# The low part of a projection weight block in eight operations of one K tile instead of four of two

## The chip, the cores and the metric

The kernel runs on one core of one Trainium2 chip. Measured is device time in microseconds of one execution of the program on that core. A chip has TensorE (PE, the matrix engine), VectorE (DVE), ScalarE (ACT), GpSimd (POOL) and SyncE (SP, which here only issues DMAs); each runs its own list of instructions in order, and they meet through semaphores.

## The reference

It is one inference step of a two-layer decoder trunk, for a prompt of 1024 positions and for 8 samples of 4 positions, which share all weights. Per layer: RMSNorm, one input projection from 1024 to 3592 columns, four token mixers beside one another (S5, HGRN2, mLSTM, retention), their gated outputs side by side, one output projection, and the residual:

```python
for l in range(DEPTH):                      # DEPTH = 2
    h = rmsnorm(x, norm_w[l])
    proj = jnp.einsum('bld,de->ble', h, w_in[l]).astype(f32)
    ...
    mixed = jnp.concatenate([s5_out * jax.nn.silu(s5_g), hg_out * jax.nn.silu(hg_g),
                             ml_out * jax.nn.silu(ml_g), rt_out * jax.nn.silu(rt_g)], axis=-1)
    x = x + jnp.einsum('ble,ed->bld', mixed.astype(x.dtype), w_out[l])
```

All of it is float32. The change touches the input projection alone.

## The kernel before

**Passes and blocks.** The prompt is cut into two halves of 512 positions, so there are four passes n = 0 to 3 (layer n // 2, half n % 2); the odd passes take the 32 sample positions along. A pass goes through 14 blocks of the input projection, each 256 columns wide (ml_ifg 264), in the order of the table BLOCKS; 4 x 14 = 56 blocks in all. `make_plan` writes down one order of steps for the whole kernel, and every engine walks through the same list and does its own share of each step.

**The split product.** TensorE multiplies in the type fp32r, and a projection is made of three products so as to keep float32's precision: the weights are split into a high part `whi` and a low part `wlo`, the rows into `hhi` and `hlo`, and for each K tile (128 of the 1024 input features; KT = 8 of them) the kernel adds hhi times whi, hhi times wlo and hlo times whi (lines 2270 to 2280). A block whose columns are channels ("ch") has the weights as the stationary operand and is done in pieces of up to 512 positions (line 2275); a "tok" block has the rows as the stationary operand and is done in pieces of 128 positions (line 2280). In the odd passes a "tok" block begins with the piece of the 32 sample positions, which multiplies the raw float32 weights `wraw` (line 2267). In the profile the trace prints the operands of the two lines 2275 and 2280 as out<-stationary,moving or the reverse; `whi`, `wlo`, `hhi` and `hlo` tell them apart.

**Who makes the parts.** ACT loads a block of weights by DMA into one of two slots of `wraw` (line 1149) and copies it as one operation into `whi` (line 1132, 128 x 2048, about 1.9 us); POOL subtracts, `wlo = wraw - whi`, in `split_low` (line 1088). Both go one block ahead of TensorE: `split_after` puts them at the first piece of the block before. `whi` and `wlo` have two slots each, so POOL first waits for the last piece of two blocks back, then for `whi`:

```python
                for g in range(4):
                    ks = slice(2 * g, 2 * g + 2)
                    nc.gpsimd.tensor_tensor(wlo[:, hslot[b], ks, 0:width], wraw[:, wslot[b], ks, 0:width],
                                            whi[:, hslot[b], ks, 0:width].bitcast(F32), ALU.subtract).then_inc(*wlo_done.inc(b + (g,)))
```

**Who waits for them.** TensorE waits for `wlo_done` in the first piece of a block, ahead of every second K tile (line 2263), also where this first piece is the sample piece, which doesn't read `wlo`. ACT waits for the last `wlo_done` of a block before it loads the next weights into that slot of `wraw` (line 1144, in `load_until`).

**What else POOL does.** In the order of the plan it computes `rstd` of a tile of rows for RMSNorm (lines 1097 and 1099; DVE's L1521 scales the rows with it, TensorE's L2245 transposes them, DVE's L1587 makes `hlo`), and `rs`, the scale of the head norm of a chunk of 128 positions (lines 1110 and 1113; DVE's L2195 multiplies `y` with it, after which TensorE's L2564 transposes `y`). Both are a short operation and a power. L1989, L2002 and L2010 are DVE's operations in the HGRN mixer; L1560 is one of the ml branch.

## Time and profile before

| | |
|---|---|
| median of 3 runs | 1610.68 us (1610.04 to 1617.34) |
| profiled execution, first to last instruction | 1609.6 us |
| its own time beside that span | not given apart; the span stands for it |
| mean granted TensorE clock | 0.919 |
| PE, PEld, DVE, ACT, POOL busy | 1387.8, 1214.1, 883.0, 524.2, 394.0 us |
| low parts on POOL (line 1088) | 224 operations, 297.1 us |
| high parts on ACT (line 1132) | 56 operations, 107.2 us |
| three products, line 2280 | 3 x 896 matmuls, 274.6 + 264.8 + 264.7 us |
| three products, line 2275 | 3 x 672 matmuls, 230.7 + 219.7 + 219.6 us |

How to read it: the times of an engine are what its instructions took; instructions of different engines overlap, and matmuls overlap one another on TensorE. In a row that ends in brackets, as [1.00 <-POOL wlo L1088], the engine stood idle for so many us before the instruction, and what follows the arrow ended this. The duration of a DVE or POOL operation includes the time in which it has begun and stands still. A row xN merges N instructions in a row.

### The profile page before, as it was taken

What the parts mean: (1) busy time and instruction counts of PE and PEld (TensorE: products, weight loads), DVE (VectorE), ACT (ScalarE), POOL (GpSimd) and SP (SyncE); (2) the same over time, 40 slices, a digit from 0 to 9 for tenths busy, and PEclk for the clock granted to TensorE, in tenths of its full rate; (3) what the DMA queues carried; (4) which work ended last, traced back from release to release, by engine and by line L of the source; (5) the groups of instructions that cost most, each with busy time, mean ns of one, the idle gap of its engine ahead of it and who ended that gap; (6) DMA issues with size and microseconds to landing.
All of it is one profiled execution on the core that took longest, in us unless ns stands there. A gap on an engine that the chain in (4) does not pass through costs nothing. (4 is left out here: it accounts for less than half of the span.)

```text
span 1609.6 us, 31327 instructions
## 1 busy us (share of the span) xinstructions
PE 1387.8 (86%) x12391; PEld 1214.1 (75%) x12391; DVE 883.0 (55%) x2652; ACT 524.2 (33%) x1093; POOL 394.0 (24%) x404
## 2 busy tenths in 40 slices
PE   3666899989897898898999989998989899789777
PEld 2566699788776787886777869877878798778546
DVE  5985736463795426455646442647365444644544
ACT  4335433333323422321443233233532433321011
POOL 4232233421001333140210144252200333231001
PEclk9888999979898999897999989998999999889879
DMA  6132123422233432372313323242313314359101
GB/s 183 59 98 68 53 81 105 138 75 90 65 107 107 112 74 76 94 127 44 106 65 95 117 77 107 82 152 67 115 50 113 106 56 120 137 82 201 54 9 57
DMA packets 167177, 149.83 MB, mean 93 GB/s; under 512 B 63440, under 2 KB 155352, under 8 KB 165240
## 3 DMA queue, kind: packets, MB, share of 16 engines
q1 hardware_dynamic: 96312, 76.38, 17.4%
q10 hardware_dynamic: 70720, 71.44, 15.4%
q8 instruction: 100, 1.64, 0.4%
q14 instruction: 45, 0.37, 0.1%
HBM read 124.42 MB, written 23.37 MB: 92 GB/s over the span
## 5 line engine op out<-in xcount | busy, mean ns | idle before, releaser
L1088 POOL TENSOR_TENSOR wlo<-wraw,whi 128x512 fp32r<-128x512 f32 (+1 forms) x224 | 297.1, 1357 | 434.0 <-ACT whi L1132 434.0
L2280 PE MATMUL psum<-whi,hhi 128*128 128x256 f32 (+1 forms) x896 | 274.6, 306 | 40.9 <-DVE r L1545 20.3
L2280 PE MATMUL psum<-wlo,hhi 128*128 128x256 f32 (+1 forms) x896 | 264.8, 296 | 0.0
L2280 PE MATMUL psum<-whi,hlo 128*128 128x256 f32 (+1 forms) x896 | 264.7, 295 | 0.0
L2275 PE MATMUL psum<-hhi,whi 128*128 128x288 f32 (+2 forms) x672 | 230.7, 343 | 2.9 <-DVE hlo L1587 1.6
L2280 PEld LDWEIGHTS psum<-whi,hhi 128*128 128x128 f32 x896 | 183.4, 205 | 49.2 <-issue 46.2
L2275 PE MATMUL psum<-hlo,whi 128*128 128x288 f32 (+2 forms) x672 | 219.7, 327 | 0.0
L2275 PE MATMUL psum<-hhi,wlo 128*128 128x288 f32 (+2 forms) x672 | 219.6, 327 | 0.0
L2280 PEld LDWEIGHTS psum<-wlo,hhi 128*128 128x128 f32 x896 | 183.3, 205 | 0.7 <-issue 0.5
L2605 PE MATMUL psum<-wraw,mixT 128*128 128x256 f32 x768 | 180.4, 395 | 4.0 <-DVE xo L2205 4.0
L2280 PEld LDWEIGHTS psum<-whi,hlo 128*128 128x128 f32 x896 | 182.6, 204 | 0.0
L1110 POOL TENSOR_SCALAR rs<-mv 128x4 f32<-128x4 f32 (+1 forms) x54 | 10.4, 192 | 665.6 <-DVE mv L2171 665.1
L2605 PEld LDWEIGHTS psum<-wraw,mixT 128*128 128x128 f32 x768 | 150.5, 199 | 27.1 <-DVE xo L2205 5.1
L1132 ACT ACTIVATE whi<-wraw 128x2048 fp32r<-128x2048 f32 (+1 forms) x56 | 107.2, 1915 | 115.1 <-PE psum L2275 44.0
L2275 PEld LDWEIGHTS psum<-hhi,whi 128*128 128x128 f32 x672 | 128.5, 191 | 18.3 <-issue 6.7
L2275 PEld LDWEIGHTS psum<-hhi,wlo 128*128 128x128 f32 x672 | 128.5, 191 | 11.8 <-issue 3.0
L2275 PEld LDWEIGHTS psum<-hlo,whi 128*128 128x128 f32 x672 | 128.1, 191 | 10.6 <-issue 0.2
L2168 DVE BATCH_NORM_STATS2 stats<-psum 128x6 f32<-128x64 f32 (+1 forms) x144 | 22.3, 217 | 105.9 <-PE psum L2526 105.9
L2526 PE MATMUL psum<-r,ST 128*128 128x64 f32 (+1 forms) x384 | 69.5, 285 | 3.8 <-issue 3.5
L1545 DVE SCALAR_TENSOR_TENSOR r<-th,psum 128x256 f32<-128x256 f32 (+3 forms) x72 | 24.9, 351 | 72.9 <-ACT th L1219 71.7
L2526 PEld LDWEIGHTS psum<-r,ST 128*128 128x128 f32 x384 | 58.0, 202 | 5.6 <-issue 5.3
L1989 DVE TENSOR_TENSOR r<-r 128x256 f32<-128x256 f32 (+1 forms) x134 | 51.6, 456 | 15.2 <-PE psum L2437 15.1
(351 smaller groups left out, 2277.5 us busy)
## 6 DMA issues: line engine op xcount, KB each, us to landing
wraw<-in_w_in ACTq DMA_DIRECT2D x50, 1024.0 KB, 5.4
wraw<-in_w_out ACTq DMA_DIRECT2D x14, 1024.0 KB, 5.4
x<-xo SPq DMA_DIRECT2D x48, 128.0 KB, 2.3
r<-x SPq DMA_DIRECT2D x10, 512.0 KB, 5.4
r<-in_c_rot SPq DMA_DIRECT2D x4, 1088.0 KB, 6.9
wraw<-in_w_in ACTq DMA_DIRECT2D x4, 1056.0 KB, 6.0
r<-WTm SPq DMA_DIRECT2D x4, 1024.0 KB, 12.7
r<-VTm SPq DMA_DIRECT2D x4, 1024.0 KB, 4.8
```

What stands on the lines that cost most here:

```text
L1088: nc.gpsimd.tensor_tensor(wlo[:, hslot[b], ks, 0:width], wraw[:, wslot[b], ks, 0:width], whi[:, hslot[b], ks, 0:width].bitcast(F32), ALU.s ...
L1110: nc.gpsimd.tensor_scalar(rs[0:T, :], mv[0:T, :, 1], EPS if s[0] == "rt" else 4 * EPS, 4.0, ALU.add, ALU.mult).then_inc(*pool_done.inc())
L1132: nc.scalar.activation(whi[:, hslot[b], :, 0:width], wraw[:, wslot[b], :, 0:width], ACT.Copy).then_inc(*whi_done.inc(b))
L1545: nc.vector.scalar_tensor_tensor(gate_of[name[:2]][0:ln, at, c], th[0:ln, i, c], 1.0, src, ALU.add, ALU.mult).then_inc(*(bank.free.inc(k) ...
L1989: nc.vector.tensor_tensor(e, x, x[:, :, at - 1:at].broadcast_to([P, 2 * T // blk, blk]), ALU.subtract).then_inc(*(dve_done.inc() if w else ...
L2168: nc.vector.bn_stats(stats[0:T, h, :], src[:, h, :]).then_inc(*dve_done.inc())
L2275: mm = nc.tensor.matmul(bank.t[:, 0:c.stop - c.start], w[:, sl, kt, k[2] * P:(k[2] + 1) * P], x[:, kt, c], start=first, stop=last)
L2280: mm = nc.tensor.matmul(bank.t[:, 0:width], x[:, kt, c], w[:, sl, kt, 0:width], start=first, stop=last)
L2526: mm = nc.tensor.matmul(o, stt[0:T, h, 0:T], v(h), start=br == "ml", stop=True)
L2605: mm = nc.tensor.matmul(bank.t[0:r, 0:256], mixT[:, row, k[2] * P:k[2] * P + r], wraw[:, wslot[b], kt, 0:256], start=kt == 0, stop=kt == 7)
```

## The change

`split_low` makes eight subtractions of one K tile each in the place of four of two, with a signal after each; TensorE waits ahead of every K tile of a block's first piece; ACT waits for the eighth signal instead of the fourth. The elements computed are the same.

```diff
--- before.py
+++ after.py
@@ -655,7 +655,7 @@
         y_out = [signal(f"y_out{s}", [k for k in final_tiles[:NCH] if tslot[k] == s], 16) for s in range(2)]
         wr_in = [signal(f"wr_in{s}", [k for k in w_loads if wslot[k] == s], 16) for s in range(2)]
         whi_done = signal("whi_done", in_blocks)
-        wlo_done = signal("wlo_done", [b + (g,) for b in in_blocks for g in range(4)])
+        wlo_done = signal("wlo_done", [b + (g,) for b in in_blocks for g in range(KT)])
         th_keys = [k for k in pieces if BLOCK[k[1]][4] == "av"]
         th_done = signal("th_done", th_keys)
         xo_in = [signal(f"xo_in{s}", [k for k in out_pieces if oslot[k] == s], 16) for s in range(3)]
@@ -1083,8 +1083,8 @@
                     pool.wait_ge(*PB[bank_of[last_piece[prev]]].full.at(last_piece[prev]))
                 pool.wait_ge(*whi_done.at(b))
                 width = BLOCK[b[1]][2]
-                for g in range(4):
-                    ks = slice(2 * g, 2 * g + 2)
+                for g in range(KT):
+                    ks = slice(g, g + 1)
                     nc.gpsimd.tensor_tensor(wlo[:, hslot[b], ks, 0:width], wraw[:, wslot[b], ks, 0:width],
                                             whi[:, hslot[b], ks, 0:width].bitcast(F32), ALU.subtract).then_inc(*wlo_done.inc(b + (g,)))
 
@@ -1141,7 +1141,7 @@
                         act.wait_ge(*PB[bank_of[(prev[0], prev[2], tiles_of(prev[0])[-1])]].full.at((prev[0], prev[2], tiles_of(prev[0])[-1])))
                     else:
                         act.wait_ge(*whi_done.at(prev))
-                        act.wait_ge(*wlo_done.at(prev + (3,)))
+                        act.wait_ge(*wlo_done.at(prev + (KT - 1,)))
                         sample = prev + (NCH,)
                         if sample in pieces:
                             act.wait_ge(*PB[bank_of[sample]].full.at(sample))
@@ -2259,8 +2259,8 @@
                                     u = ("norm", n, t, g)
                                     pe.wait_ge(*PB[bank_of[u]].free.at(u))
                         for kt in range(*((0, 4) if part[0] == "mm" else (4, KT)) if long_piece(k) else (KT,)):
-                            if kt % 2 == 0 and k == pieces_of_block(*b)[0]:
-                                pe.wait_ge(*wlo_done.at(b + (kt // 2,)))
+                            if k == pieces_of_block(*b)[0]:
+                                pe.wait_ge(*wlo_done.at(b + (kt,)))
                             if tiled(k):
                                 width = BLOCK[b[1]][2] // 4
                                 for g in range(4):
```

On POOL, from the first low parts on (the first block's; `rstd<-ssq` and `rstd<-rstd,epow` are the next row statistic, `rs` the head scales). Before:

```order
L1088 TENSOR_TENSOR wlo<-wraw,whi 128x2x256 x4
L1097 TENSOR_SCALAR rstd<-ssq 128x1
L1099 TENSOR_TENSOR rstd<-rstd,epow 128x1
L1088 TENSOR_TENSOR wlo<-wraw,whi 128x2x256 x12
L1088 TENSOR_TENSOR wlo<-wraw,whi 128x528 x4
L1088 TENSOR_TENSOR wlo<-wraw,whi 128x2x256 x4
L1110 TENSOR_SCALAR rs<-mv 128x4
L1113 TENSOR_TENSOR rs<-rs,epow 128x4
```

and after the change:

```order
L1088 TENSOR_TENSOR wlo<-wraw,whi 128x256 x8
L1097 TENSOR_SCALAR rstd<-ssq 128x1
L1099 TENSOR_TENSOR rstd<-rstd,epow 128x1
L1088 TENSOR_TENSOR wlo<-wraw,whi 128x256 x24
L1088 TENSOR_TENSOR wlo<-wraw,whi 128x264 x8
L1088 TENSOR_TENSOR wlo<-wraw,whi 128x256 x8
L1110 TENSOR_SCALAR rs<-mv 128x4
L1113 TENSOR_TENSOR rs<-rs,epow 128x4
```

The order is the same; each group of four became one of eight, and an operation's two runs of 256 columns became one. What stood behind four operations stands behind eight.

On TensorE, the start of the second block (hg_i of pass 0, three matmuls to a K tile). Before:

```order
L2280 MATMUL psum<-whi,hhi 128x256 [waits proj1_free,proj0_free,proj2_free,wlo_done,whi_done]
L2280 MATMUL psum<-wlo,hhi 128x256
L2280 MATMUL psum<-whi,hlo 128x256
L2280 MATMUL psum<-whi,hhi 128x256
L2280 MATMUL psum<-wlo,hhi 128x256
L2280 MATMUL psum<-whi,hlo 128x256
L2280 MATMUL psum<-whi,hhi 128x256 [waits wlo_done]
L2280 MATMUL psum<-wlo,hhi 128x256
L2280 MATMUL psum<-whi,hlo 128x256
L2280 MATMUL psum<-whi,hhi 128x256
L2280 MATMUL psum<-wlo,hhi 128x256
L2280 MATMUL psum<-whi,hlo 128x256
```

and after the change:

```order
L2280 MATMUL psum<-whi,hhi 128x256 [waits proj1_free,proj0_free,proj2_free,wlo_done,whi_done]
L2280 MATMUL psum<-wlo,hhi 128x256
L2280 MATMUL psum<-whi,hlo 128x256
L2280 MATMUL psum<-whi,hhi 128x256 [waits wlo_done]
L2280 MATMUL psum<-wlo,hhi 128x256
L2280 MATMUL psum<-whi,hlo 128x256
L2280 MATMUL psum<-whi,hhi 128x256 [waits wlo_done]
L2280 MATMUL psum<-wlo,hhi 128x256
L2280 MATMUL psum<-whi,hlo 128x256
L2280 MATMUL psum<-whi,hhi 128x256 [waits wlo_done]
L2280 MATMUL psum<-wlo,hhi 128x256
L2280 MATMUL psum<-whi,hlo 128x256
```

The matmuls are the same; a wait for a low part stands at each K tile instead of each second one. Nothing moves on DVE, ACT and SP; ACT's waits stand where they stood and mean the same point, the last low part of a block.

## Rows read from the trace of the kernel before

**Rows 1.** The page: busy us of each engine, share of the span, instructions.
```profile
PE 1387.8 (86%) x12391; PEld 1214.1 (75%) x12391; DVE 883.0 (55%) x2652; ACT 524.2 (33%) x1093; POOL 394.0 (24%) x404
```

**Rows 2.** Forms on POOL: xcount, busy us, mean ns, idle us before.
```profile
L1088 POOL TENSOR_TENSOR wlo<-wraw,whi 128x512 fp32r<-128x512 f32 x208 | 274.3, 1350 | 415.5 <-ACT whi L1132 415.5
...
L1095 POOL TENSOR_TENSOR ssq<-ssq,ssq_rest 128x1 f32<-128x1 f32 x5 | 0.9, 189 | 63.1 <-ACT th L1164 63.1
```

**Rows 3.** Line 1088's instructions: ns minimum/median/maximum, first and last start.
```profile
L1088 POOL TENSOR_TENSOR wlo<-wraw,whi x224: 1257/1289/2997, 24.3 to 1446.4; 128x512 fp32r<-128x512 f32 x104, 128x528 fp32r<-128x528 f32 x8
```

**Rows 4.** TensorE in order of time, hg_i, first pass: start, us, instruction.
```profile
51.25 0.29 PE L2280 MATMUL psum<-whi,hlo 128*128 128x256 f32 x1
51.38 0.28 PE L2280 MATMUL psum<-whi,hhi 128*128 128x256 f32 x1
51.49 0.28 PE L2280 MATMUL psum<-wlo,hhi 128*128 128x256 f32 x1
```

**Rows 5.** Timelines 808 to 834: POOL, TensorE, ACT around the tightest ordinary block.
```profile
809.04 6.59 POOL L1088 TENSOR_TENSOR wlo<-wraw,whi 128x512 fp32r<-128x512 f32 x4 [25.69 <-ACT whi L1132]
...
818.57 0.29 PE L2280 MATMUL psum<-whi,hhi 128*128 128x256 f32 x1
...
815.72 0.37 ACTq L1149 DMA_DIRECT2D wraw<-in_w_out  x1
...
825.77 1.09 ACT L1348 ACTIVATE r<-psum 128x512 f32<-128x512 f32 x2 [8.54 <-PE psum L2387]
```

**Rows 6.** TensorE 1254 to 1262, its idle time in brackets; then the chain.
```profile
1255.54 0.44 PE L2267 MATMUL psum<-wraw,mixT 128*32 128x66 f32 x16 [1.00 <-POOL wlo L1088]
...
1259.22 0.67 PE L2267 MATMUL psum<-wraw,mixT 128*32 128x66 f32 x16 [0.59 <-POOL wlo L1088]
...
1254.59 7.03 DMA wraw<-in_w_in
```

**Rows 7.** POOL and DVE, then windows: length, then PE busy us and count.
```profile
24.29 5.92 POOL L1088 TENSOR_TENSOR wlo<-wraw,whi 128x512 fp32r<-128x512 f32 x4 [1.92 <-ACT whi L1132]
30.30 0.19 POOL L1097 TENSOR_SCALAR rstd<-ssq 128x1 f32<-128x1 f32 x1
...
31.24 1.28 DVE L1521 SCALAR_TENSOR_TENSOR r<-r,rstd 128x1024 f32<-128x1024 f32 x1 [2.18 <-POOL rstd L1099]
...
724.63 0.43 DVE L2195 TENSOR_TENSOR y<-y,rs 128x256 f32<-128x256 f32 x1 [1.46 <-POOL rs L1113]
...
sum 155.00, PE 154.41 PEld 134.26 DVE 79.53 ACT 47.55 POOL 67.77; mean PE 38.60 PEld 33.56 DVE 19.88 ACT 11.89 POOL 16.94
```

**Rows 8.** DVE's y operations: ns minimum/median/maximum; then busy us and mean ns.
```profile
L2195 DVE TENSOR_TENSOR y<-y,rs x54: 411/426/1424, 146.1 to 1537.4; 128x256 f32<-128x256 f32 x48, 32x256 f32<-32x256 f32 x6
...
L2195 DVE TENSOR_TENSOR y<-y,rs 128x256 f32<-128x256 f32 (+1 forms) x54 | 33.9, 627 | 18.7 <-POOL rs L1113 17.2 <-issue 0.9
```

**Rows 9.** Timelines: POOL, DVE, TensorE's weight loads at 666; DVE at 258.
```profile
667.92 5.12 POOL L1088 TENSOR_TENSOR wlo<-wraw,whi 128x512 fp32r<-128x512 f32 x4
...
668.08 1.38 DVE L2195 TENSOR_TENSOR y<-y,rs 128x256 f32<-128x256 f32 x1 [0.22 <-POOL rs L1113]
...
670.93 0.29 PEld L2564 LDWEIGHTS psum<-const,y 128*128 128x128 f32 x2 [4.58 <-issue]
...
258.68 1.77 DVE L1560 TENSOR_TENSOR r<-r 128x512 f32<-128x512 f32 x1
```

**Rows 10.** TensorE's waits: us in total, times, longest us.
```profile
PE psum L2564 <- ACT kT L1453: 22.0, 6, 5.2
```

**Rows 11.** POOL and DVE at 178; then DVE where POOL is still.
```profile
178.66 5.60 POOL L1088 TENSOR_TENSOR wlo<-wraw,whi 128x512 fp32r<-128x512 f32 x4
...
178.83 1.41 DVE L2195 TENSOR_TENSOR y<-y,rs 128x256 f32<-128x256 f32 x1 [0.16 <-POOL rs L1113]
180.17 6.05 DVE L1989 TENSOR_TENSOR r<-r 128x256 f32<-128x256 f32 x8
...
147.10 2.76 DVE L1989 TENSOR_TENSOR r<-r 128x256 f32<-128x256 f32 x8
```

## The prediction

> **What bounds the kernel now.** I read the page first: TensorE is busy 86% of the span, POOL 24%, DVE 55% [rows 1]. So a change on POOL can reach the time in three ways only: TensorE waits for a low part, something queued behind the low parts on POOL comes late, or POOL gets in the way of DVE. The views behind each follow. The profiled span is 1609.6 us and the median of the three runs 1610.68; no separate time of the profiled execution is given, so the sum is made against the span and the result is carried over by adding the 1.1 us between the two. About 0.5% of 1610, which is 8 us, is what a measurement of this kernel can tell from no change (one of the three runs lies 6.7 us above the median).
>
> **Price of one operation.** The forms of POOL [rows 2] give 189 ns for a two-input operation on one column and a mean of 1350 ns for 512 columns; the undisturbed one is 1257 ns, the median 1289 [rows 3]. A straight line through 189 at 1 column and 1257 at 512 has a slope of 2.09 ns a column, so 256 columns take 189 + 255 x 2.09 = 722 ns. Bounds: no cheaper than half, 0.63 us; no dearer than the whole, 1.26 us. I take 0.72, which lies between two measured sizes. POOL starts the next before the last has quite ended (four take 4.98 us where nothing disturbs them, not 5.03), so eight take about 5.7 us against 5.0: **+0.7 us in each of 56 blocks, 39 us of POOL time**, all of it in an engine that idles three quarters of the span.
>
> **Term 1, TensorE's waits themselves.** Its waits on the low part double, 224 to 448. A wait that is already satisfied can be read off: in the piece that begins at 50.66 us the third K tile's first matmul (51.38) carries one and follows its forerunner by 0.13 us, the next, which carries none, by 0.11 [rows 4]. Times are rounded to 0.01 and other starts in this piece are 0.12 apart with no wait, so the row bounds it at 0 and 0.02 us a wait, 0 and +4.5 over 224; I take the low side, 1 ns each, **+0.2**, as the matmuls keep their rhythm.
>
> **Term 2, low parts that come late.** The low parts are made one block ahead. The tightest ordinary block is the one whose operations run 809.04 to 815.63; TensorE wants the last pair at 818.57 [rows 5], 2.9 us later (one more block, at 906 us, leaves as little; all others more). There DVE is in the way as well, so eight operations could take 5.7 us plus twice the 1.6 us that POOL lost now, 8.9 us: done at 817.9, and the last K tile is now wanted 0.36 us after the pair was. Still hidden: 0. The other user of these signals is ACT, which sat until that last low part landed before it issued the next load, an output weight block, at 815.72 [rows 5]; its next operation but one waits 8.54 us for TensorE anyway, so what is queued behind on ACT is covered, and TensorE still has this whole block to finish before it wants the weights loaded. 0, and +2 us if that cover is gone.
> Once TensorE does wait: the sample piece of ml_ifg in the last pass is first in its block, and TensorE follows POOL in four steps, 1.00 us idle at the first, 0.59 at the last [rows 6]. That piece multiplies the raw weights and needs no low part. Now the last signal is 0.7 later but one K tile is left behind it, not two (0.2 us less, half of the 0.44 us of a step): TensorE ends it 0.5 us later. What is late next is not TensorE: the chain runs through the load of the next block, 7.03 us to 1261.62, and ACT behind it [rows 6]. 0, and +0.5 uncovered.
>
> **Term 3, what is queued behind on POOL.** Each row statistic (rstd) and head scale (rs) of POOL that is ready while low parts run waits for them. In the start phase rstd starts at 30.30, the moment the four operations end, DVE had idled 2.18 us for it [rows 7], and TensorE waits for that tile of rows: **+0.7 us on the path**. Seven more, two rstd and five rs, start right where a block of low parts ends. All lie in four stretches in which TensorE is busy for 154.41 of 155.00 us [rows 7], so they are hidden at first; one of them makes DVE's y wait 1.46 us for it at 724.63 [rows 7], near the end of its stretch and not far ahead of the next wait of TensorE, and there I let it through: +0.7. Together **+1.4**; bounds +0.7 and 8 x 0.7 = +5.6.
>
> **Term 4, the shared way to SBUF, which can cut both ways.** DVE operations that read two tiles from SBUF stand still while a low part runs. The scaling y of 128x256 takes 426 ns at the median but up to 1424 [rows 8]; 54 of them take 33.9 us, 10.9 us more than at 426. The Trainium skill, "SBUF — State Buffer", section "SBUF: two separate sides", says why: GpSimd and such a DVE operation take an exclusive lock on a port pair for a whole instruction, and the loser blocks; these rows agree.
> *Lone operations gain.* At 667.92 POOL begins four low parts right behind the pow that y waits for, y starts at 668.08 and takes 1.38 us [rows 9], 0.95 too much, and TensorE then waits for what ACT makes of it: 4.58 us of idling before its transposes [rows 9], 22.0 us in six waits in all [rows 10]. With a first operation of 0.72 us instead of 1.26, y is free 0.53 us sooner. Five of TensorE's waits end behind such a y (at 547, 641, 671, 1380 and 1415 us): **-2.5 us**, bounds 0 and -2.7. In two ml blocks (256 and 1022 us) y and a later 1.77 us operation [rows 9] are both held up and TensorE waits shortly after: 4 x 0.54 = -2.2 on DVE, of which I count half, **-1.1**.
> *Dense runs stay even.* At 178.66 the four take 5.60 us, y 1.41, and the eight L1989 behind it 6.05 [rows 11]; the same eight take 2.76 us where POOL is still [rows 11]. The difference is 3.29 us for the three of them that meet a low part, 1.1 each, and y loses 0.98: each low part stops one DVE operation for about 1.09 us, 4 x 1.09 = 4.4. With eight of them each stops one for 1.09 - 0.54 = 0.55, 8 x 0.55 = 4.4: the same, since the run has more than eight operations in it. There are nine such windows (39, 53, 80, 91, 134, 179, 487, 768 and 778 us). Where DVE comes in late, in the windows at 134 and 1263, the 0.7 us that POOL runs on stop it for 0.5 more: **+1.0** together. Bounds: all nine even out at only four stops, -2.2 each, -20; or the stop keeps a fixed part so that it is 0.65, not 0.55: +0.8 each, +7.
>
> **Sum.** +0.2 + 0 + 1.4 - 2.5 - 1.1 + 1.0 = -1.0 us. Span 1608.6, median 1609.7. **Forecast: no change, 1609.7 us.** The change works on POOL's own time and on two small effects of opposite sign.
>
> **Rivals.**
> A, *DVE is set free* (faster). If the number of stops stays what it is, four to a window, and only their length halves, DVE gets back half of what it loses. Its price: nine windows at -2.2 us is -20, about half of it on TensorE's path, with the lone ones -3.6 and the losses +2.6: 1610.7 - 11 = 1600. For it: the stops are long and many. Against: rows 11 show one stop per low part, back to back, as long as DVE has work, so more parts make more stops. (The skill's rule of the lock on the same page gives the length of a stop, not their number, and is silent between this rival and the forecast; by a half of every stop the sum would be this one, by rows 11 it is the forecast's.) It decides if the dense windows hold fewer than about six two-input operations.
> B, *short operations are dear* (slower). If 256 columns cost over 0.95 us rather than 0.72, eight take 7.6 us or more, 2.6 over the four. The place is the nine dense windows: each stop is then 0.8, 8 x 0.8 = 6.4 against 4.4, +2.0 x 9 = +18, most of it in the start phase where DVE sets the pace, say +12; the rs and rstd behind add 2.6 x 2 = +5; less 1 for the lone ones: 1610.7 + 16 = 1627. For it: nothing on this trace has that size. Against: 189 ns at one column leaves no room for a large fixed part.
> C, *TensorE loses its run-ahead at each wait*: +0.02 us x 224 = 4.5, 1614; within no change. Rows 4 speak against it.
> That the change doesn't do what it says can be left out: the order on both engines shows eight operations and a wait at each K tile.
>
> **How the numbers follow.** Forecast with C 0.86, A 0.07, B 0.07. The first covers the bounds of the sum short of their far ends and the runs' own spread, 1604 to 1616; A and B lie outside and together hold less than two in ten. So the range is 1604 to 1616. Faster 0.07, same 0.86, slower 0.07.
>
> **What would show it.** POOL's L1088 at 448 operations with a median near 0.72 us and POOL's busy time near 435 us; the y operations' maximum near 0.9 us instead of 1.42, and DVE busy a few us less; the dense window at 179 with eight L1989 and y still about 7.5 us together; rstd at about 31.0 instead of 30.30; TensorE waiting at the ml_ifg sample piece of the last pass and at no other low part. Wrong if a 256-column operation takes 0.9 us or more, if DVE's busy time falls by over 15 us, or if TensorE waits for low parts in ordinary blocks.

## The result, and the profile after

Six executions of each kernel on the same chip: 1603.61 us after (1595.95 to 1607.93), 1613.19 before (1610.04 to 1617.34). The ratio is **0.9932, interval 0.9905 to 0.9959**, so the change takes away some 11 us (the medians differ by 9.6). The forecast was 1609.7 us and no change; the measured time lies 0.4 us under its range, but the distance that counts is 11 us of gain where 1.0 was forecast. The run that was profiled is the fastest of the six (span 1594.1 us) and makes the gain look like 15.5 us; the ratio decides.

The page of the changed kernel, engines, for [rows 1], and its line 1088 and its y operations (ns minimum/median/maximum), for [rows 3, 8]:

```profile
PE 1382.4 (87%) x12391; PEld 1210.3 (76%) x12391; DVE 865.9 (54%) x2652; ACT 524.2 (33%) x1093; POOL 436.3 (27%) x628
```
```profile
L1088 POOL TENSOR_TENSOR wlo<-wraw,whi x448: 714/737/2445, 24.7 to 1431.9; 128x256 fp32r<-128x256 f32 x139, 128x264 fp32r<-128x264 f32 x11
...
L2195 DVE TENSOR_TENSOR y<-y,rs x54: 412/426/861, 143.5 to 1521.9; 128x256 f32<-128x256 f32 x48, 32x256 f32<-32x256 f32 x6
```

POOL has 42 us more to do and DVE 17 us less, more than the 15 that the prediction named as a sign of being wrong. The operation takes 737 ns at the median, priced at 722; y's total goes from 33.9 to 27.3 us, and its longest from 1424 to 861 ns. The start phase on POOL and DVE, for [rows 7]:

```profile
24.66 6.54 POOL L1088 TENSOR_TENSOR wlo<-wraw,whi 128x256 fp32r<-128x256 f32 x8 [1.93 <-ACT whi L1132]
31.28 0.19 POOL L1097 TENSOR_SCALAR rstd<-ssq 128x1 f32<-128x1 f32 x1
...
32.22 1.28 DVE L1521 SCALAR_TENSOR_TENSOR r<-r,rstd 128x1024 f32<-128x1024 f32 x1 [4.52 <-POOL rstd L1099]
```

rstd starts 0.98 us later, priced at 0.7: the eight operations take 0.62 us longer (6.54 for 5.92) and begin 0.37 later. TensorE's sample piece in the last pass, first and last of its eight steps, and the waits of TensorE (us, times, longest), for [rows 6, 10]:

```profile
1238.73 0.32 PE L2267 MATMUL psum<-wraw,mixT 128*32 128x66 f32 x8 [0.45 <-POOL wlo L1088]
...
1243.54 0.45 PE L2267 MATMUL psum<-wraw,mixT 128*32 128x66 f32 x8 [0.25 <-POOL wlo L1088]
...
PE psum L2564 <- ACT kT L1453: 17.4, 5, 4.0
...
PE psum L2267 <- POOL wlo L1088: 2.7, 8, 0.4
```

The waits before L2564 are 4.6 us shorter. The dense window that was at 178 and the lone y that was at 668, for [rows 11, 9]:

```profile
176.05 6.91 POOL L1088 TENSOR_TENSOR wlo<-wraw,whi 128x256 fp32r<-128x256 f32 x8
...
176.22 0.85 DVE L2195 TENSOR_TENSOR y<-y,rs 128x256 f32<-128x256 f32 x1 [0.16 <-POOL rs L1113]
177.00 6.59 DVE L1989 TENSOR_TENSOR r<-r 128x256 f32<-128x256 f32 x8
...
662.26 5.71 POOL L1088 TENSOR_TENSOR wlo<-wraw,whi 128x256 fp32r<-128x256 f32 x8
...
662.41 0.84 DVE L2195 TENSOR_TENSOR y<-y,rs 128x256 f32<-128x256 f32 x1 [0.22 <-POOL rs L1113]
...
664.73 0.29 PEld L2564 LDWEIGHTS psum<-const,y 128*128 128x128 f32 x2 [4.04 <-issue]
```

In the dense window y and the eight L1989 take 0.85 + 6.59 = 7.44 us, where they took 1.41 + 6.05 = 7.46: even, as predicted. The lone y takes 0.84 instead of 1.38, and TensorE idles 4.04 instead of 4.58, 0.54 less, also as predicted. Where, then, do 11 us come from?

**A place that the sum had nearly left out.** Both traces hold the same 12391 matmuls in the same order, so the start of one in the kernel before less its start in another says how far ahead the other is there. Between 1018 and 1045 us of the kernel before, the changed kernel gains 5.5 us. One other stretch of this length gives as much, 80 to 107 us in the start phase (6.0), but of that lead only 2.6 us are left at 160 us. In the kernel before, the timelines of POOL, DVE and TensorE there (an ml block):

```profile
1022.50 5.65 POOL L1088 TENSOR_TENSOR wlo<-wraw,whi 128x512 fp32r<-128x512 f32 x4
...
1022.65 1.41 DVE L2195 TENSOR_TENSOR y<-y,rs 128x256 f32<-128x256 f32 x1 [0.22 <-POOL rs L1113]
...
1025.23 1.77 DVE L1560 TENSOR_TENSOR r<-r 128x512 f32<-128x512 f32 x1
1027.03 1.66 DVE L1568 TENSOR_TENSOR r<-r 128x512 f32<-128x512 f32 x1
...
1031.74 1.54 PE L2526 MATMUL psum<-r,ST 128*128 128x65 f32 x8 [2.86 <-issue]
```

and in the changed kernel:

```profile
1012.19 6.69 POOL L1088 TENSOR_TENSOR wlo<-wraw,whi 128x256 fp32r<-128x256 f32 x8
...
1012.35 0.85 DVE L2195 TENSOR_TENSOR y<-y,rs 128x256 f32<-128x256 f32 x1 [0.22 <-POOL rs L1113]
...
1014.36 0.69 DVE L1560 TENSOR_TENSOR r<-r 128x512 f32<-128x512 f32 x1
1015.08 1.11 DVE L1568 TENSOR_TENSOR r<-r 128x512 f32<-128x512 f32 x1
...
1019.25 1.08 PE L2526 MATMUL psum<-r,ST 128*128 128x65 f32 x8 [0.66 <-issue]
```

Three operations had stood still here and are shorter: y by 0.56 us, L1560 by 1.08, L1568 by 0.55, 2.19 us in all. TensorE's wait falls from 2.86 to 0.66 us, by just that much. The other 3 us lie behind the wait. Windows over the wait and what follows it (stretch, length, busy us and count of PE, PEld, DVE, ACT, POOL, then the granted clock), before and after:

```profile
1028.00:1041.00 13.00, 10.14 (x66) 9.56 (x64) 6.98 (x27) 2.36 (x8) 1.43 (x3) 0.74 0.47 163
```
```profile
1015.00:1028.00 13.00, 12.34 (x103) 11.34 (x102) 7.56 (x29) 3.50 (x17) 5.17 (x7) 1.00 0.50 163
```

Before, TensorE stands 2.86 us and its clock then falls to half (1.2 GHz) for 6.8 us, which makes 0.74 in the mean. After, it stands 0.66 us, keeps the full 2.4 GHz (1.00), and starts 103 matmuls in the 13 us instead of 66.

### The profile page after: what moved, and what is told of

It reads as the page before. It is cut to its first block and busy times, and to the rows that moved or that the text cites. A ratio compares the mean times of both kernels' runs of the same rounds, so it can differ in the third digit from the quotient of the medians.

```text
span 1594.1 us, 31551 instructions
## 1 busy us (share of the span) xinstructions
PE 1382.4 (87%) x12391; PEld 1210.3 (76%) x12391; DVE 865.9 (54%) x2652; ACT 524.2 (33%) x1093; POOL 436.3 (27%) x628
## 5 line engine op out<-in xcount | busy, mean ns | idle before, releaser
L1088 POOL TENSOR_TENSOR wlo<-wraw,whi 128x256 fp32r<-128x256 f32 (+1 forms) x448 | 339.3, 794 | 408.2 <-ACT whi L1132 408.2
L1110 POOL TENSOR_SCALAR rs<-mv 128x4 f32<-128x4 f32 (+1 forms) x54 | 10.4, 193 | 634.1 <-DVE mv L2171 633.5
L1989 DVE TENSOR_TENSOR r<-r 128x256 f32<-128x256 f32 (+1 forms) x134 | 52.7, 464 | 17.7 <-PE psum L2437 17.6
```

Source lines behind the costliest of these rows:

```text
L1989: nc.vector.tensor_tensor(e, x, x[:, :, at - 1:at].broadcast_to([P, 2 * T // blk, blk]), ALU.subtract).then_inc(*(dve_done.inc() if w else ...
```

## The experiments

All ratios are to the kernel before on the same chip, with 95% intervals. "At 1018" is the gain between 1018 and 1045 us of the kernel before, from matmul starts as above, in the one profiled run of each; "at 50" that between 50 and 100 us, in the start phase. The runs differ by some 3 us (once, e9 between 700 and 720 us, by 7) in places that nothing touches, so these two are local evidence, and the ratio is the verdict.

| run | what differs from the kernel before | median us | ratio | DVE busy | at 1018 | at 50 |
|---|---|---|---|---|---|---|
| the change | 8 operations, 8 waits | 1603.61 | 0.9932 [0.9905, 0.9959] | 865.9 | 5.5 | 3.3 |
| e11_again | the same kernel again | 1600.10 | 0.9920 [0.9893, 0.9947] | 865.6 | 4.9 | 4.5 |
| e1_ops8_sig4 | 8 operations, 4 waits | 1600.56 | 0.9917 [0.9895, 0.9940] | 867.1 | 6.4 | 3.6 |
| e2_ops4_wait8 | 4 operations, 8 waits | 1613.93 | 0.9997 [0.9976, 1.0018] | 881.2 | 0.0 | 0.4 |
| e3_ops16 | 16 operations | 1597.80 | 0.9902 [0.9872, 0.9931] | 853.4 | 5.5 | 2.6 |
| e4_ops2 | 2 operations | 1623.97 | 1.0064 [1.0038, 1.0089] | 903.9 | 0.0 | -0.5 |
| e5_noread | low parts filled, not read | 1560.13 | 0.9674 [0.9650, 0.9699] | 808.0 | 6.4 | 11.7 |
| e6_dense | 8 in ten dense blocks | 1611.24 | 0.9997 [0.9974, 1.0019] | 876.7 | -1.3 | 4.1 |
| e7_lone | 8 in twelve lone blocks | 1602.88 | 0.9935 [0.9910, 0.9961] | 872.6 | 4.9 | -0.8 |
| e8_two | 8 in blocks 3 and 4 | 1608.13 | 0.9974 [0.9954, 0.9993] | 880.6 | 0.0 | 2.9 |
| e9_first | first of 4 halved, twelve blocks | 1605.23 | 0.9960 [0.9935, 0.9985] | 876.7 | 2.6 | -0.6 |
| e10_ml | 8 in rt_v and rt_g of each pass | 1604.44 | 0.9963 [0.9943, 0.9983] | 874.2 | 4.9 | -0.3 |
| e12_lone16 | 16 in twelve lone blocks | 1603.42 | 0.9938 [0.9913, 0.9964] | 868.6 | 4.9 | -0.6 |
| f1_rest | 8 in the other 44 blocks | 1613.12 | 0.9999 [0.9981, 1.0016] | 877.5 | 0.0 | 2.6 |
| f2_noread_lone | filled in twelve lone blocks | 1596.31 | 0.9888 [0.9865, 0.9911] | 859.2 | 6.4 | 0.9 |
| f3_noread_dense | filled in ten dense blocks | 1580.26 | 0.9807 [0.9773, 0.9840] | 844.7 | -1.3 | 13.3 |
| f4_ywait4 | POOL waits for y, 4 operations | 1601.86 | 0.9928 [0.9906, 0.9951] | 874.8 | 5.0 | -0.6 |
| f5_ywait16 | POOL waits for y, 16 | 1594.58 | 0.9901 [0.9877, 0.9926] | 851.4 | 6.4 | 4.8 |
| f6_ywait8 | POOL waits for y, 8 | 1598.12 | 0.9916 [0.9893, 0.9940] | 863.0 | 6.1 | 3.2 |

"Lone" are the twelve blocks (8, 11, 20, 25, 26, 32, 38, 39, 49, 52, 53, 54 in order of the 56) in which few DVE operations meet the low parts, ten of them with a y that stands still; e9 takes the twelve blocks with such a y instead, that is 7 and 18 (dense) for 38 and 52. "Dense" are the ten (1 to 5, 7, 18, 29, 30, 47) where they meet a long run of DVE. In e5, f2 and f3 the low parts are filled with zeros, in the blocks named, so the product loses its hhi·wlo term there and POOL reads nothing.

**Operations or waits?** e1 has the change's operations with the old signals, e2 the reverse.

```diff
 e1: one K tile per operation; only every second signals
+ low.then_inc(*(wlo_done.inc(b + (g // 2,)) if g % 2 else pool_done.inc()))
 e2: TensorE waits ahead of each K tile, on the old four signals
- if kt % 2 == 0 and k == pieces_of_block(*b)[0]:
+ if k == pieces_of_block(*b)[0]:
```

> Eight subtractions to a block as in the change, but signalled in pairs, so that TensorE waits at every second K tile as before. Theory 1 (each low part that runs stops one DVE operation until it ends, the stop is half as long with half the columns, and what DVE hands on in the middle of a window is early): the same time as the changed kernel, 0.990 to 0.996 of before. Theory 2 (finer signals let TensorE start sooner): the time of before, within 0.3%. Theory 3 (the gain is chance in TensorE's clock from one execution to the next): within 0.3% of before too, with the granted clock of before, 0.919.

> Four subtractions of two K tiles as before, but TensorE waits ahead of every K tile (for the pair that holds it). Theory 1: the time of before within 0.3%. If 224 more waits cost 0.02 us each it would be +4.5 us, 1.003.

e1 is the change within its interval, e2 no change: all of it comes from the operations. TensorE's starts in e2, in the piece of [rows 4]:

```profile
50.98 0.28 PE L2280 MATMUL psum<-whi,hhi 128*128 128x256 f32 x1
51.10 0.28 PE L2280 MATMUL psum<-wlo,hhi 128*128 128x256 f32 x1
...
51.34 0.28 PE L2280 MATMUL psum<-whi,hhi 128*128 128x256 f32 x1
```

The first and the last shown carry a wait and, like the middle one, start 0.11 to 0.12 us behind their forerunners (50.87 and 51.22): a satisfied wait costs nothing that these rows can show, and 224 more of them nothing that the ratio can (interval -3.9 to +2.9 us).

**Fewer and more operations.** e3 halves each operation again (columns 0 to 127 and 128 to 255 of a K tile), e4 takes four K tiles in one.

```diff
 e3
+ for cs in (slice(0, width // 2), slice(width // 2, width)):
 e4
- for g in range(4):
-     ks = slice(2 * g, 2 * g + 2)
+ for g in range(2):
+     ks = slice(4 * g, 4 * g + 4)
```

> Sixteen subtractions of half a K tile (128 columns), a signal after each K tile. By the line through the two sizes now measured (0.189 us at 1 column, 0.734 at 256) one takes 0.46 us, with 16 of them some 6.8 us a block against 5.6. Theory 1: stops of about 0.28 us, lone ones cheaper by another 0.26, hand-offs in the middle of a window earlier again: 2 to 6 us faster than the changed kernel, 0.987 to 0.993 of before, less what the later last low parts cost (1.2 us for rstd in the start phase). Theory 2: no further gain, as TensorE's waits are those of the changed kernel. Theory 3: as before within 0.3%.

> Two subtractions of four K tiles (1024 columns, by the same line about 2.33 us each), two signals. Theory 1: stops of about 2.1 us, twice those of before, so the gain of the change with the other sign and larger: 10 to 25 us slower, 1.006 to 1.015. Theory 2: TensorE waits more at the sample pieces and in the tight blocks, 1 to 5 us. Theory 3: as before within 0.3%.

Line 1088 of e3, then of e4 (ns minimum/median/maximum), and y in e4 (busy us, mean ns):

```profile
L1088 POOL TENSOR_TENSOR wlo<-wraw,whi x896: 445/459/4555, 24.8 to 1435.4; 128x128 fp32r<-128x128 f32 x168, 128x132 fp32r<-128x132 f32 x12
```
```profile
L1088 POOL TENSOR_TENSOR wlo<-wraw,whi x112: 2333/2393/4084, 24.1 to 1457.2; 128x1024 fp32r<-128x1024 f32 x104, 128x1056 fp32r<-128x1056 f32 x8
...
L2195 DVE TENSOR_TENSOR y<-y,rs 128x256 f32<-128x256 f32 (+1 forms) x54 | 47.0, 871 | 18.0 <-POOL rs L1113 16.8 <-issue 0.6
```

The sign follows the length of an operation: 2393 ns costs 0.6%, 1289 is the kernel before, 737 gains 0.7%, 459 gains 1.0%, not clearly more than the change (the intervals of e3 and e11 overlap). With sixteen operations DVE does get time back in the dense window of [rows 11]: y and the eight operations behind it take 0.57 + 4.90 us, where they took 7.46 with four and 7.44 with eight. The likely reason, which no run tests by itself: some ten DVE operations are there to be stopped, so sixteen short ones no longer find one each. In e3, POOL, then DVE:

```profile
177.73 8.65 POOL L1088 TENSOR_TENSOR wlo<-wraw,whi 128x128 fp32r<-128x128 f32 x16
...
178.39 4.90 DVE L1990 TENSOR_TENSOR r<-r 128x256 f32<-128x256 f32 x8
```

**No reading at all.** How much is there to gain in the two places?

```diff
- nc.gpsimd.tensor_tensor(wlo[...], wraw[...], whi[...].bitcast(F32), ALU.subtract)
+ nc.gpsimd.memset(wlo[...].bitcast(F32), 0.0)
 f2, f3: the same, in the twelve lone or the ten dense blocks only
```

> The four low parts of a block are not computed: POOL fills each pair of K tiles of wlo with zeros, an operation that reads nothing (about 0.5 us by the fill of 5440 columns in 4.62 us, against 1.26), signals and waits as before. Theory 1 (DVE's two-input operations stand still while POOL reads SBUF): y never takes over 0.6 us, DVE's busy time falls by most of the 65 us that it now stands still, 15 to 30 us faster, 0.981 to 0.991 of before. If what DVE loses is cover everywhere and the gain of the change comes from elsewhere: 0 to 5 us from the earlier rstd and rs alone.

> Low parts left out in the twelve lone blocks alone: POOL fills them with zeros and reads nothing. All low parts so replaced gave 0.967. Theory 1 with lone stops worth most: -14 to -22 us, 0.986 to 0.991, twice what halving their stops gave. If lone stops are small and dense ones large: -4 to -10 us.

> Low parts left out in the ten dense blocks alone. They hold about 40 of the 65 us that DVE stands still. If dense runs lie on the path and eight short stops only replace four long ones, this gives -20 to -35 us, 0.978 to 0.988, though eight operations gave nothing; if dense runs lie beside TensorE's work, -5 to -12 us.

e5, line view: busy us, mean ns:

```profile
L2194 DVE TENSOR_TENSOR y<-y,rs 128x256 f32<-128x256 f32 (+1 forms) x54 | 22.9, 424 | 12.9 <-POOL rs L1112 12.8 <-DVE S_rt L2182 0.2
...
L1088 POOL MEMSET wlo<- 128x512 f32 (+1 forms) x224 | 107.9, 526 | 491.5 <-ACT whi L1131 491.5
```

A POOL operation that only writes stops no y (424 ns each). With fills the kernel is 3.3% shorter, 52 us where 15 to 30 were expected; f3 gives 1.9% of it (31 us) in the dense blocks, f2 1.1% in the lone ones. These are upper bounds of what the reads cost: a fill takes 526 ns and a subtraction 1289, so POOL is also done some 3 us a block sooner (e5 is 12 us ahead at 73 us), and TensorE multiplies zeros; no run parts these from the reads. So the dense blocks hold more than the lone ones, and yet the change gets almost nothing there; next.

**Dense or lone?**

```diff
+ def parts_of(b):
+     return 8 if in_blocks.index(b) in (...) else 4
- for g in range(4):
+ for g in range(parts_of(b)):
 and the same number in wlo_done, in ACT's wait and in TensorE's
```

> Eight subtractions and eight waits in the ten blocks alone whose low parts run beside a dense run of DVE's two-input operations (second to sixth block, then 7, 18, 29, 30 and 47 counted from 0); four in the other 46. The prediction on record has these even out, +1 us. Theory 1 with hand-offs in the middle of a window: DVE ends its run at the same time, but what it hands to TensorE before the end comes up to 2.2 us sooner: 4 to 8 us faster, 0.995 to 0.9975. In the trace: TensorE restarts near 96.4 us, not 100.0.

> Eight subtractions and waits in the twelve blocks alone in which DVE meets the low parts with one to three operations, y mostly (8, 11, 20, 25, 26, 32, 38, 39, 49, 52, 53, 54 counted from 0); four in the other 44. The prediction on record has -3.6 us for these; Theory 1 the same or somewhat more, as TensorE's clock also stays high where it waits less: 3 to 8 us faster, 0.995 to 0.998. Together with the dense blocks about the whole gain of the change.

> The complement of the lone blocks: eight operations and waits in all 44 blocks but the twelve lone ones. If the parts add up (change 0.992 to 0.993, lone blocks 0.9935): 0.998 to 1.001, with the -5 us that the dense blocks' trace shows in TensorE's idle time eaten by later rstd and by the clock. If the dense blocks really give 5 us that their own timing missed: 0.995 to 0.998.

> Eight subtractions and waits in two blocks alone, hg_g and ml_ifg of the first pass, whose low parts run at 80 and 91 us. Theory 1: all before 80 us as in the kernel before, TensorE restarts at 96.4 to 97.0 us in the place of 100.0, and some of these 3 us are still there at 190 us. If the start phase of the change gained by its earlier blocks: TensorE restarts at 100.0 as before. Total 0.997 to 1.000.

e7 alone gives as much as the change, 10.5 us (interval 6.3 to 14.5; 3 to 8 were expected); e6 and f1, which hold every dense block, give nothing (4 to 8 were expected of e6). One thing stays open: at 50 the start phase is 2.6 to 4.8 us shorter wherever blocks 3 and 4 have eight operations or sixteen (change, e11, e1, e3, e6, e8, f1, f5, f6), and not in e2, e4, e7, e9, e10, e12 or f4. TensorE waits there in the middle of a dense run for a tile of DVE's; in the kernel before and in the changed one:

```profile
100.02 0.55 PE L2280 MATMUL psum<-whi,hhi 128*128 128x256 f32 x1 [5.45 <-DVE r L1538]
```
```profile
96.44 0.36 PE L2280 MATMUL psum<-whi,hhi 128*128 128x256 f32 x1 [1.06 <-DVE r L1538]
```

This run is not even. The 44 DVE operations that start between 76 and 112 us take 33.5 us in the kernel before, 31.3 in the change, e11 and e8, and what stands in their middle is done sooner. POOL stands still here too: its operations take about 1.25 us each instead of 0.74. In the kernel before and in the changed one:

```profile
79.80 6.76 POOL L1088 TENSOR_TENSOR wlo<-wraw,whi 128x512 fp32r<-128x512 f32 x4 [21.84 <-ACT whi L1132]
```
```profile
80.61 9.44 POOL L1088 TENSOR_TENSOR wlo<-wraw,whi 128x256 fp32r<-128x256 f32 x8 [22.28 <-ACT whi L1132]
```

The dense windows at 768 and 778 give DVE 1.2 us together, and TensorE's wait that ends at 789.97 is 1.0 to 1.1 us shorter in the change, e11, e1, e6 and f1 and as long as before in e7, e10 and f4. e8 keeps its gain (4.2 us, interval 1.1 to 7.4), e6 and f1 show none of theirs in their time, though their intervals would just allow 3 us. A part of the loss can be seen: in the change and e8 the lead of 4.8 and 5.3 us at 120 us is 2.6 and 3.2 at 160; the rest was not found.

**The first operation only, and the blocks rt_v and rt_g.** e9 halves only the first of the four operations, in the twelve blocks whose y stands still; e10 has eight operations in rt_v and rt_g of each pass (blocks 10, 11, 24, 25, 38, 39, 52, 53), whose low parts meet the ml mixer.

```diff
 e9
+ def cuts(b):
+     return (0, 1, 2, 4, 6, 8) if in_blocks.index(b) in (...) else (0, 2, 4, 6, 8)
 e10
+     return tuple(range(9)) if in_blocks.index(b) in (...) else (0, 2, 4, 6, 8)
```

> In the twelve blocks whose low parts start right behind the power that y waits for, the first pair of K tiles alone is done as two operations, the other three pairs as one each (five operations, five waits); the other 44 blocks as before. Theory 1y (the gain sits in y's shorter stop): y's longest falls to 0.86 us as in the change, and most of the gain of the twelve lone blocks is here, -6 to -10 us, 0.994 to 0.996. Theory 1m (it sits in the operations behind y, that is in the ml blocks, and in what TensorE's clock gives back there): -1 to -4 us, 0.9975 to 0.9995.

> Eight operations and waits in eight blocks alone, the two ml blocks of each pass beside which DVE runs L1560, L2155, L2158 and y (10, 11, 24, 25, 38, 39, 52, 53 counted from 0). Theory 1m: TensorE's wait of 2.86 us near 1031 us falls under 1 us and the granted clock of the 13 us around it rises from 0.74 to 0.95 or more; -5 to -9 us in all, 0.994 to 0.997. Theory 1y: only the y of three of them counts, -1 to -2 us, 0.9985 to 0.9995.

e9's y operations, all but one form:

```profile
L2199 DVE TENSOR_TENSOR y<-y,rs x54: 411/426/859, 146.6 to 1538.1; 128x256 f32<-128x256 f32 x48, 32x256 f32<-32x256 f32 x6
```

e9 gives 6.4 us (2.4 to 10.5) with y as short as in the change. At 1018 it gains 2.6, not 4.9: y is 0.85 us long there, but L1560, with long low parts behind the first, takes 1.24 and L1568 1.67. e10 gives 6.0 us (2.7 to 9.2) and 4.9 of them are seen at 1018 (block 39).

**y out of the way.** POOL does the power for y and then starts its low parts at once, just as DVE starts y. Here it waits until y is done; the operations stay four of two K tiles.

```diff
+ if scaled:
+     pool.wait_ge(*y_done.at(scaled[-1]))      # ahead of the low parts
  nc.gpsimd.tensor_tensor(rs[...], rs[...], epow[...], ALU.pow).then_inc(*rs_done.inc(s))
+ scaled.append(s)
```

> Four operations and four waits as before, but POOL begins a block's low parts only when the y that its last power was for has been scaled, so y is never stopped; the low parts start some 0.5 us later in the twelve blocks behind a power. Theory 1y (y's stop is what the lone blocks pay): y at most 0.6 us, -6 to -10 us, 0.994 to 0.996, as much as splitting the first pair (0.996) or more. Theory 1m: -2 to -4 us, 0.9975 to 0.999, since the later operations are stopped as before or are met later.

Its y operations, the low parts at the lone place of [rows 9], and TensorE's wait of the ml block:

```profile
L2199 DVE TENSOR_TENSOR y<-y,rs x54: 411/425/427, 146.4 to 1527.8; 128x256 f32<-128x256 f32 x48, 32x256 f32<-32x256 f32 x6
...
663.53 4.97 POOL L1091 TENSOR_TENSOR wlo<-wraw,whi 128x512 fp32r<-128x512 f32 x4 [0.72 <-DVE y L2199]
...
1023.40 1.08 PE L2530 MATMUL psum<-r,ST 128*128 128x65 f32 x8 [1.24 <-issue]
```

No y stands still (427 ns at most), POOL starts 0.72 us later, and the time is 11.6 us shorter (7.9 to 15.2): as much as the change, with not one operation shorter. It is 11.0 us of DVE's time that y gets back (33.9 to 22.9), but the two equal numbers are no proof that each y lies on the path. The starts of the matmuls say where it counts: 5.0 us at 1018, 0.97, 0.94, 0.95, 0.60 and 0.92 us at the waits of TensorE that end at 547, 641, 671, 1380 and 1415, each behind a y, and nothing around five of the twelve y (179, 200, 487, 907 and 1301). Windows of f4 and of e9 over the wait of that ml block, for the clock:

```profile
1015.00:1028.00 13.00, 11.76 (x101) 11.32 (x102) 8.81 (x24) 3.73 (x17) 6.99 (x5) 1.00 0.43 161
```
```profile
1028.00:1041.00 13.00, 10.94 (x85) 10.58 (x84) 8.88 (x27) 3.22 (x12) 5.40 (x6) 0.87 0.45 163
```

**Both together, and sixteen in the lone blocks.** Do the gains add?

> Sixteen operations of half a K tile, and POOL begins a block's low parts only after the y of its last power. Sixteen operations alone gave 0.9902, with twelve y still stopped for 0.15 to 0.2 us each; that leaves 1 to 3 us: 0.988 to 0.991. If the stops of the operations behind y matter as well, and the shorter starts help them, 0.985 to 0.988.

> The changed kernel with the same wait of POOL for y. The change gave 0.992 to 0.993 with twelve y stopped for 0.43 us; taking this away is 12 x 0.43 = 5 us if each lies on the path as with four operations (12 x 0.98 = 11.8 us, measured 11.6): 0.988 to 0.991. If y's stop and the shorter operations are the same gain counted twice: 0.992 to 0.993.

> Sixteen operations of half a K tile, a signal to each K tile, in the twelve lone blocks alone; four in the other 44. Theory 1: stops of 0.28 us there in the place of 0.53 and 1.07: 1 to 4 us faster than the same blocks with eight (0.9935), 0.990 to 0.993. If what counts is being under the length of the waits that TensorE's clock forgives, no more than with eight, 0.993 to 0.995.

> The changed kernel itself once more, beside the two above: 0.990 to 0.996, as measured and as with the signals in pairs. If the gain was chance it is within 0.3% of before.

Not that it shows: eight operations with the wait (f6, 0.9916) is the change again, sixteen with it (f5, 0.9901) is e3, and sixteen in the lone blocks (e12) is e7. Added up, the change and f4 would give 0.986; that is outside f6's interval, while a few us more than the change would be inside. So the gain of the change and of f4 is in the main the same one. Best is 0.9901 to 0.9902, f5 or e3: 0.7 to 1.3% below the kernel before, below the change perhaps.

**The place at 1018, over all kernels.** Worked out from the matmul starts, in us gained on the kernel before; 1018 to 1030 holds TensorE's wait and the matmul that ends it, 1030 to 1045 what comes right behind, 1045 to 1060 its next wait, which ends at 1056.78:

```
                                     1018-1030   1030-1045   1045-1060
the change                                2.5         3.1        -0.5
e3                                        2.4         3.1        -2.0
e11 (the change again)                    1.8         3.1        -2.0
e7, e10                                   1.8         3.1        -1.5
e12                                       1.8         3.1         0.0
e1, f5                                    3.3         3.1        -2.0
e5                                        3.3         3.1        -1.5
f2                                        3.3         3.1         0.0
f6                                        3.0         3.1        -1.8
f4                                        1.9         3.1        -1.5
e9 (only the first operation shorter)     1.1         1.5         0.0
e4 (two operations in block 39)           0.0         0.0        -1.4
e2, e8 (block 39 as before)               0.0         0.0         0.0
f1 (block 39 as before)                   0.0         0.0        -0.5
e6, f3 (block 39 as before)               0.0        -1.3        -0.2
```

Every kernel that gets y, L1560 and L1568 of this one block through sooner is 4.9 us or more ahead at 1045, by whatever means, e9 half, and the five that leave the block alone gain nothing. e4 loses nothing there: its y takes 2.52 us for 1.41, but the three operations together take as long as before (4.83 for 4.84). By 1060 the lead has shrunk, to 5.0 us in the change, 2.9 in e11 and 3.4 in e7, e10 and f4. In most traces a stretch of 3.4 us at half clock falls there, which costs 1.5 us. And 0.53 us goes at TensorE's wait that ends at 1056.78, in the change, e11, e1, f1 and f6 and not in e7, e10 and f4: with eight operations the low parts beside it run on 0.6 us longer and stop one more DVE operation (L2155 of before, 0.17 us, 0.69 in f1).

How long TensorE stands in this one wait doesn't say by itself what the clock does. Behind 2.86 us (before, e2, e8, f1) it was at half for 6.8 us. It was so too in e4 behind 1.73 us, with another stop of 1.21 us ahead, and in e6 and f3 behind 1.60, with 3.4 us at half clock ahead; in e9 behind 2.06 us only for 3.4 us, and behind 1.24 (f4) or less not at all. In e7, e10, e11 and e12 3.4 us at half clock come ahead of the wait: TensorE gets there later and finds nothing to wait for, and that is why e11 gains 1.8 us there and the change, the same kernel, 2.5. In e7 the 13 us that hold the wait's place show it, a busy PE and 0.87 of the clock:

```profile
1015.00:1028.00 13.00, 13.00 (x103) 12.74 (x102) 8.11 (x22) 3.84 (x17) 6.81 (x9) 0.87 0.50 163
```

**The clock over all executions.** One trace can't say what the clock gives in total, since the stretches at half clock lie elsewhere in each; the means over all executions can. The mean granted clock of the kernel before is 0.917 to 0.918 on each chip, that of e2, e6 and f1, which gain nothing, 0.917 to 0.918 as well, and that of the change 0.920, e11 0.921, e1 0.919, e7 0.922, f4 0.921. What the clock is short of 1, times the execution's time, is 133 to 134 us before, and less by 5.6 us (2.5 to 8.7) in e11, 4.8 (0.7 to 8.9) in e1, 8.4 (3.2 to 13.6) in e7 and 6.8 (3.5 to 10.1) in f4. This is an estimate from above of what the clock gives back, as part of the time at half clock TensorE stands idle anyway: some 5 to 8 of the 10 to 12 us. In e10 it is 1.8 us (-1.6 to 5.2), which leaves open whether the clock has a share in its 6.0.

## Why the prediction was wrong

*The step that failed is in Term 4: "In two ml blocks (256 and 1022 us) ... 4 x 0.54 = -2.2 on DVE, of which I count half, -1.1."* The mechanism was right and the size wrong, and TensorE's clock had no place in the sum at all. The wait behind the block at 1022, half of that term, was to end 0.55 us sooner. It ends 2.2 us sooner in the change and 1.6 in f4. Not two operations with half a stop each (1.1 us) stand before it but three with four (2.19), since L1560 became free altogether and L1568 was held up too; and all of it reached the wait, not half. Behind the wait 3.1 us more are gained, because the clock doesn't fall there, of which most kernels give 1.5 back before 1060. The block at 256 gave 0.3 to 2.2 us between 240 and 300 us in the change, e11, e1, e7 and e10, against -0.7 to 0.5 where it has four operations or two (e2, e4, e6, e8, f1).

The wait of 2.86 us was in the trace of before, and so was the 0.74 behind it; I had costed the wait without looking at the window after it. Over all executions the clock stands for some 5 to 8 of the 11 us, by the estimate above, which may be the larger part of the miss.

*The five lone y, "-2.5":* right, at four of the five places beyond doubt. Taken at each wait alone (how much sooner the matmul behind it starts, less the same for the matmul ahead of it), e7 gains 0.54, 0.54, 0.48, 0.54 and 0.39 us at 547, 641, 671, 1380 and 1415, 2.5 together, and e1 2.6. Where the block keeps its four operations nothing is gained (e10 at 547 and 671: 0.0 and -0.1; at 641 and 1380, where it has eight, 0.53), and e4 loses 1.05 to 1.14 at each. Only 1415 scatters: e11, with eight there, loses 1.0, and e2, with four, 1.4. The change itself gains 1.5 and 1.6 at 641 and 1380, which e1, e7 and e10 don't repeat. What comes of it at the end is another matter: between 672 and 700 the change, e11 and e7 lose 0.5, 2.8 and 0.5 us again.

*The dense windows, "even":* right in the windows at 134, 179, 487 and 1263, to 0.15 us of DVE's time, and in the totals (e6 0.9997, f1 0.9999); not in those at 80 and 91 (2.1 us less together) and at 768 and 778 (1.2 us less); what those at 39 and 53 gain (0.1 and 0.7 us) is not clear of the scatter (e2: 0.2 and 0.4). The +1.0 for late arrivals is the right size in the wrong place, by luck: the windows at 134 and 1263 cost DVE 0.15 and 0.13 us, but TensorE's waits that end at 287 and 1057 end 0.53 us later each.

*DVE's time.* The prediction said "a few us less" and called a fall of over 15 us a sign of being wrong: it fell by 17.1, 10.4 of them with the lone blocks alone (e7; e2, which changes nothing there, differs by 1.8). The lone y and the ml blocks had been counted at 4.9.

*Term 1, +0.2:* right (e2). *The price of one operation:* 0.722 was 0.737, POOL 436.3 us for "near 435". *Term 2, 0:* right; TensorE waited for a low part in the sample piece only. *Term 3, +1.4:* rstd came 0.98 us later, TensorE too (37.14 for 36.16 us), but by 73 us it was level again, so nothing of it was left; nor is the wait at 736.75, behind the y at 724.63, any longer.

*The rivals.* A, "DVE is set free", named nearly the right time, 1600, by luck: it put 10 us into the dense windows, and e6, with eight operations in all of them, gives DVE 6.3 us back and the kernel nothing. B and C are refuted by 737 ns and by e2. The chances were the second fault: 0.07 for faster rested on a sum of small terms, each with its size known to a half, and none with what the clock may add.

What is not settled: the waits behind y and the one at 1031 account for about 5 us of the change's 11 (2.5 and 2.2 or more), the clock for 5 to 8, and the late arrivals take 1.1. The clock's part rests on means, it holds only as an upper bound, and which of the shorter waits it comes from is seen at 1031 alone. The start phase gives 2.6 us by 160 in the change and e8 keeps 4.2 in its time, but e7, without it, measures as much as the change. The intervals are 3 to 4 us each way, so the parts can't be divided further.

## What to carry to other kernels

Where two engines hold each other up, look first at what the *first* operation behind a hand-over has to sit out: POOL started long work in the moment in which it released DVE, and either shorter operations (e7) or one wait for DVE's short operation (f4) won about 0.7%. In a dense run half as long operations made about as many more stops and won nothing in the time (e6, f1), though the fills did (f3). When a change shortens a wait of TensorE, read the granted clock of the window behind that wait before pricing it, and follow the lead past the next waits: here 2 us of waiting carried 3 us of slow matmuls with them, and in most of the kernels half of these were lost again within 15 us. Compare the start of a matmul in both traces at one wait at a time; it separates 0.5 us where whole profiles differ by several.

## What the runs showed of the hardware

A POOL subtraction of 128 partitions takes 459 ns for 128 columns, 737 for 256, 1289 for 512 and 2393 for 1024: the same 2.16 ns a column from each size to the next and 0.18 us fixed (medians). While it runs, a DVE operation that reads two tiles from SBUF can stand still to its end: y takes 1.41 us for 0.43 behind an operation of 1289 ns and 0.85 behind one of 737. A POOL fill of 526 ns, which reads nothing, held none of the 54 y up (e5). It goes the other way too: in the dense run at 80 us eight POOL operations take 9.44 us, at the lone place at 662 us 5.71. With sixteen operations DVE still loses time to them, at 853.4 us against 808.0 with fills.

One kernel's executions spread by more than its profile suggests: the kernel before ran from 1603.80 to 1622.28 us in 20 executions of one chip, at a mean granted clock of 0.911 to 0.920, and the effect looked for is 11 us. Where the stretches at half clock lie differs from run to run of one kernel (the change and e11 around 1031 us), so one pair of profiles (here 15.5 us apart) is no measure of a change of this size.
